# GpSimd writes each weight slot's low part in pieces of 512 columns

## The reference, cut to what matters

```python
# first_block, twice: a mixer (an HGRN2 scan in layer 0, latent attention in layer 1),
# attention over a memory of 256 tokens, and a gated feed-forward with a short convolution
h = rms_norm(x, mix_norm_g[layer])
z = h @ w_in                                   # hg_w_in or mla_w_in
x = x + concat([mixer(z), memory_attention(z, mem)]) @ w_out[layer]
u = conv(rms_norm(x, ffn_norm_g[layer]) @ w_up[layer]) + conv_b
x = x + (silu(u[..., :2816]) * u[..., 2816:]) @ w_down[layer]
# second_block, once: three branches off one projection
p = (rmsnorm(x, norm_g) * (1 + sc) + sh) @ w_in + b_in
y_a = (a_b * short_conv(a_c * a_x) * silu(a_z)) @ w_br_a
y_f = (fourier_mix(f_u) * silu(f_z)) @ w_br_f
y_c = (neighbourhood_attention(q, k, v, k_ctx, v_ctx, rpb) * silu(c_z)) @ w_br_c
out = rmsnorm(x + gt * ((sig(g_a)*y_a + sig(g_f)*y_f + sig(g_c)*y_c) @ w_out), final_g)
```

## Time and profile before

| | |
|---|---|
| median of three runs | 1850.66 us (1849.72 to 1851.76) |
| span of the profiled execution (the profiler's own time of it) | 1846.5 us |
| TensorE busy | 1809.0 us, 98% |
| VectorE busy | 931.2 us, 50% |
| ScalarE busy | 731.6 us, 40% |
| GpSimd busy | 690.4 us, 37%, in 217 instructions |
| of it L1201 | 609.0 us in 144 instructions, 4229 ns each |
| HBM traffic | 92 GB/s on average |

### The profile page before, as it was taken

The page is one execution under the profiler, slowest core; times in us unless marked ns, Lnnn a source line. Parts: engine busy times, 40 slices in busy tenths (PEclk is TensorE's granted clock), DMA queues, the critical chain, the costliest instruction groups (busy, mean ns, idle before and its releaser), DMA issues.

```text
span 1846.5 us, 24566 instructions
## 1 busy us (share of the span) xinstructions
PE 1809.0 (98%) x9607; PEld 1472.4 (80%) x9607; DVE 931.2 (50%) x1303; ACT 731.6 (40%) x963; POOL 690.4 (37%) x217
## 2 busy tenths in 40 slices
PE   9999989999999999999999999999999999999998
PEld 6799857888888887566888888888887788888886
DVE  5366874555652116664455655235327734413564
ACT  4152163555554224553355555323214542221423
POOL 1214803444443443330344443444334334443332
PEclk9999999999999999999999999999999999999999
DMA  8632202232222231120232222323421122323211
GB/s 299 245 137 69 70 1 69 93 110 92 91 91 87 94 121 60 36 69 24 69 114 91 91 93 91 109 102 107 82 90 46 46 88 83 117 91 106 77 69 69
DMA packets 28186, 170.35 MB, mean 92 GB/s; under 512 B 3024, under 2 KB 5328, under 8 KB 11728
## 3 DMA queue, kind: packets, MB, share of 16 engines
q1 hardware_dynamic: 24720, 151.20, 23.8%
q10 hardware_dynamic: 3392, 18.09, 2.9%
HBM read 167.18 MB, written 2.10 MB: 92 GB/s over the span
## 4 chain that ended last, share of the span: by engine, by line
PE 76%; issue 11%; DVE 5%; POOL 3%; ACT 3%; DMA 0%; ACTq 0%; POOLq 0%; DVEq 0%
PE ps L397 47%; PE ps L826 12%; POOL wlo L1201 3%; PE ps L682 1%; PE ps L1092 1%; PE ps L1075 1%; PE ps L551 1%; PE ps L553 1%; PE ps L552 1%; PE ps L1104 1%; PE ps L1102 1%; PE ps L1103 1%; PE ps L417 1%; PE ps L917 1%; PE ps L419 1%
## 5 line engine op out<-in xcount | busy, mean ns | idle before, releaser
L1201 POOL TENSOR_TENSOR wlo<-wraw,whi 128x2048 fp32r<-128x2048 f32 (+3 forms) x144 | 609.0, 4229 | 1035.2 <-ACT whi L1316 1011.5
L397 PE MATMUL ps<-hh,whi 128*128 128x512 f32 x1344 | 526.5, 392 | 1.2 <-DVE wlo L1879 0.4
L397 PE MATMUL ps<-hh,wlo 128*128 128x512 f32 x1344 | 523.2, 389 | 0.0
L397 PE MATMUL ps<-hl,whi 128*128 128x512 f32 x1344 | 523.1, 389 | 0.0
L1316 ACT ACTIVATE whi<-wraw 128x2048 fp32r<-128x2048 f32 (+3 forms) x149 | 265.2, 1780 | 361.0 <-PE ps L397 289.0
L397 PEld LDWEIGHTS ps<-hh,whi 128*128 128x128 f32 x1344 | 252.3, 188 | 56.4 <-issue 2.5
L397 PEld LDWEIGHTS ps<-hh,wlo 128*128 128x128 f32 x1344 | 252.3, 188 | 52.7
L397 PEld LDWEIGHTS ps<-hl,whi 128*128 128x128 f32 x1344 | 252.4, 188 | 52.1 <-issue 0.5
L2185 DVE SCALAR_TENSOR_TENSOR scr<-ps,vec,scr 128x510 f32<-128x510 f32 (+1 forms) x176 | 120.2, 744 | 93.1 <-ACT scr L1525 93.1
L826 PE MATMUL ps<-gh,whi 128*128 128x512 f32 x352 | 137.7, 391 | 1.3 <-DVE gl L2200 1.3
L826 PE MATMUL ps<-gh,wlo 128*128 128x512 f32 x352 | 137.0, 389 | 0.0
(11 more groups left out here) (472 smaller groups left out, 2814.1 us busy)
## 6 DMA issues: line engine op xcount, KB each, us to landing
wraw<-in_w SPq DMA_DIRECT2D x63, 1024.0 KB, 4.9
wraw<-in_w0b SPq DMA_DIRECT2D x26, 1024.0 KB, 4.9
wraw<-in_w1o SPq DMA_DIRECT2D x26, 1024.0 KB, 4.9
wraw<-in_wd SPq DMA_DIRECT2D x32, 704.0 KB, 4.0
ada<-in_wada ACTq DMA_DIRECT2D x12, 1024.0 KB, 8.6
xtok<-in_x SPq DMA_DIRECT2D x4, 512.0 KB, 8.6
out<-ytok SPq DMA_DIRECT2D x4, 512.0 KB, 4.0
wraw<-in_w SPq DMA_DIRECT2D x3, 576.0 KB, 3.9
```

Of the source, the lines that this page charges most:

```text
L397: last = mm(o, l, r, start=(k == 0 and n == 0), stop=(k == K - 1 and n == 2))
L1201: nc.gpsimd.tensor_tensor(wlo[:, s % 2, 0:wd], wraw[:, s % 2, 0:wd], whi[:, s % 2, 0:wd].bitcast(F32), ALU.subtract).then_inc(lo_ready, 1)
```

## The change

The low part of a slot is made by several instructions of at most 512 columns: four for 2048 columns, three for 1408 and 1152, two for 1024. They follow one another with no wait between, and the last one adds to `lo_ready`. VectorE's low parts stay whole.

```diff
+LOW = 512
@@ in block.gpsimd, lo(s, i=None, wd=SLOT) @@
                 pool.wait_ge(hi_ready, n)
-                nc.gpsimd.tensor_tensor(wlo[:, s % 2, 0:wd], wraw[:, s % 2, 0:wd], whi[:, s % 2, 0:wd].bitcast(F32),
-                                        ALU.subtract).then_inc(lo_ready, 1)
+                for a in range(0, wd, LOW):
+                    b = min(a + LOW, wd)
+                    last = nc.gpsimd.tensor_tensor(wlo[:, s % 2, a:b], wraw[:, s % 2, a:b], whi[:, s % 2, a:b].bitcast(F32),
+                                                   ALU.subtract)
+                last.then_inc(lo_ready, 1)
```

## The result

The changed kernel takes 1856.29 us (median of 7 runs, 1853.38 to 1856.70) where the kernel before, beside it, takes 1849.72 (1848.35 to 1851.76): a ratio of 1.0030, 95% interval 1.0021 to 1.0040. A second set of runs gave 1854.64 (11 runs, 1853.05 to 1856.74) against 1849.89, a ratio of 1.0027 (1.0018 to 1.0036). It is slower, by 6.6 and 4.8 us; 1856.5 was predicted.

A forecast was written before the change was run, and what follows sets the result against it. TensorE, busy 1809.0 of 1846.5 us, was taken to bound the kernel. Gains of 5.0 us against losses of 10.75 add 5.8 us to the span; with 4.2 us from span to median that predicts 1856.5 us, range 1848 to 1864.

The forecast's parts named there:

- GpSimd's price: Splitting a full 2048-column low part into four instructions costs GpSimd 0.35 us more, bounds 0 and 0.6 us.
- Turns: At piece boundaries VectorE and GpSimd alternate, one instruction each; each SBUF-only VectorE instruction delays the low part 0.25 to 0.55 us.
- The rival without turns: VectorE never gets in between pieces; nothing won, just-in-time slots pay the bare price: 5.5 us slower, 1856.2 us, chance 0.2.
- pieces cost nothing extra: Rival: pieces are free but take turns; losses 6.3 us against 6 of gains, 1851 us, no measurable change, chance 0.25.
- off the path by its own row: Reading of the profile before: GpSimd, busy 37%, is not on the path that sets the time.
- `mkn` near 819: L2319 from 815.37 waits only for piece 2, so TensorE's 1.22 us wait on mkn goes: 1.2 us won.
- `pr`: L2445 at 1386.09 is done at 1387.25 instead of 1389.27, so TensorE's wait goes whole: 1.3 us won.
- `mqn`: TensorE's wait on mqn near 743 goes: 0.7 us won.
- the table chain: Sine tables, stalls at 693.37 and 702.02: each chained instruction pays a piece; 0.5 us won, bounds -1 and +2.
- the softmax after 819: Stall at 825.95 of two short prm instructions shortens the softmax chain some 1.5 us; waits on prm give 1.0 us.
- Slot 144: Inverse transform's sums: L2518, L2519, L2520 take turns with pieces 2 to 4; low part ends 1729.5, not 1727.13: 2.3 us lost.
- Slots 21 and 73: Just-in-time low parts where VectorE's instructions now take turns between the pieces: each 1.3 us late, 2.6 us lost together.

The follow-up runs named there:

- the first experiment: Changed kernel with the low part left whole in the twenty slots it reaches just in time, the rest in pieces: 1842.93 us, ratio to before 0.9957.
- the six-slot kernel: Pieces of 512 columns in slots 61, 64, 65, 69, 70 and 119 alone, every other low part one instruction: 1844.53 us, ratio to before 0.9971.

## Why the prediction was right

The mechanism was right, in both its halves and nearly slot by slot. That the first median, 1856.29 us, came within 0.2 us of the figure is luck all the same: the work itself costs 4.6 us and not 5.8, and half-clock stretches, which no step counted, made up the rest.

**GpSimd's price.** Predicted 0.35 us per full slot, measured 0.42 (slots 20 and 72: +0.42 each). Pieces start 1.25 us apart, where I had 1.23. The low parts' own busy time rose by 102 us and not by 44: the 44 left out the turns, which count as GpSimd's now.

**Turns.** They take one each, back to back, with no wait and no signal between the pieces: chain and slots above show it at every place. The rival without turns gave the same time, 1856.2, and is refuted by the traces and by the first experiment, which by it couldn't have been faster than before. That pieces cost nothing extra is refuted by slot 20. Of the signs named in advance, L2518 (here L2522) fell to 1.78 us and not to 1.7 or less, the waits on `wlo` at slots 21, 73, 106 and 108 are 0.5 to 0.9 us and not 1 or more, and the one on `mkn` is down to 0.4 and not gone. One reading was loose: "off the path by its own row" goes by GpSimd's busy share, while the page of before has L1201 with 3% in its chain that ended last. They are twelve low parts between 1480 and 1722 us, and in that stretch my list of losses lacked slots 124 to 130. The Trainium skill (SBUF — State Buffer, section "Who interferes with whom") says that two SBUF inputs or a two-port mode take the pair of ports shared with GpSimd for a whole instruction, and that an instruction with at most one SBUF input outside those modes does not contend. The trace agrees with the second half too: L2150, with one input in PSUM, takes 0.69 us beside the last piece of slot 21, as it does with GpSimd idle (0.68 at 327.34 before), where L1878 and L1860 took 1.73 and 1.77.

**Gains, 5.0 predicted, 5.7 found.** `mkn` near 819 1.2 and 1.40; `pr` 1.3 and 1.36; `mqn` 0.7 and 1.00; `mkn` near 756 0.3 and 0.36; the table chain 0.5 and 0.85, four turns in each stretch as told; the softmax after 819 1.0 and 0.71, the one I had too high.

**Losses, 10.75 predicted, 10.3 found.** Slot 144 2.3 and 2.28. Slots 106, 108, 110 and 112 0.7, 0.7, 0.45, 0.75 and 0.64, 0.68, 0.45, 0.61; 100 to 104 0.6 and 0.75; 140 0.7 and 0.77; 12 0.6 and 0.72. Two terms were off. Slots 21 and 73 lost 0.90 each and not 1.3: the low part grew by 1.32 us as worked out, but TensorE came 0.42 later from slot 20 and the low part's start did not, so it had that much more in hand. Two late slots in a row don't simply add. And slots 10 and 150 lost nothing (150 did lose 0.33 in the kernel with only twenty slots in pieces), 124 to 130 lost 0.36 that I had not listed, 134 0.39 for 0.25.

**The sum and the clock.** Without the clock the change costs 4.6 us, where I had 5.8. The 4.2 us that I put between span and median were two things: a run's time lies some 2.0 us above its own span, and the profiled execution of before (span 1846.5) was one of the fastest, some 1848.5 by this, at a mean clock of 0.997. Taking the two together did no harm, since it led back to the median. What came on top is half-clock stretches, of which I had counted none: two in the trace of before, three in the second of the changed kernel, four in the first (near 164, 280, 847 and 1734). The one behind slot 144's wait is in both traces of the changed kernel; the first has the one at 164 beside it, and a median 1.65 us higher than the second set's.

## What to carry to other kernels

Cutting a GpSimd instruction in pieces doesn't free VectorE, it hands out turns: each VectorE instruction that contends waits out one piece, and each turn delays what waits for GpSimd by that instruction's own length, on top of 0.14 us per added piece. So cut only where a VectorE stall ends in a TensorE wait (here six slots, 7.5 us below before with pieces of 256), leave whole what is just in time, and look for both kinds in the trace before choosing one size for all. Count the slack per slot at the point where TensorE comes, since a stall one slot earlier adds to it.

## What the runs showed of the hardware

TensorE's clock has stretches of some 3.4 us, in two traces one of 6.8, at the lower of its two levels (granted 0.5, 1.2 GHz). Which of them a run has differs from run to run: eleven of the twelve traces have one near 280, behind a gap of 2.2 us between two matmuls' starts that all twelve have, eight have one near 840, and three one near 164, though all twelve have the same gap of 2.1 us before it. The trace of before has two, near 277 and 840, which its 40 slices of 46 us average away. With slot 144's wait of 2.65 us TensorE stood still, and then worked at half clock: 11 matmuls in 4 us instead of 19. Windows of the first profiled execution of the changed kernel, and of the kernel with slots 69 and 119 whole, whose wait was 2.68 us (columns: us, then busy us and count of PE, PEld, DVE, ACT and POOL, granted clock, DMA share, GB/s):

```profile
1734.00:1738.00 4.00, 4.00 (x11) 3.12 (x12) 3.41 (x4) 0.90 (x2) 4.00 (x3) 0.57 0.76 244
```

```profile
1734.00:1738.00 4.00, 4.00 (x19) 3.31 (x18) 2.45 (x3) 1.06 (x1) 4.00 (x4) 1.00 0.74 260
```

Of the six traces with this wait (2.6 to 4.1 us) five have such a stretch behind it, of the six others none. With 256 columns a second one follows the 2.6 us wait near 1288, and in the six-slot kernel one follows the 2.8 us wait at 712, where the kernel before waits 3.2 us and has none. So such waits make it likelier and don't settle it; one costs 1.6 us. The times of a kernel's runs fall in groups about that far apart: the second set of the changed kernel has three runs at 1853.1, five at 1854.5 to 1854.9 and three at 1856.5 to 1856.7. In the 21 runs of before beside the first experiments the mean time at a mean clock of 0.995, 0.996 and 0.997 was 1851.1, 1849.5 and 1848.1 us, in the two later sets 1851.1 to 1851.3, 1849.7 to 1849.8 and 1848.8 to 1848.9. So most of the spread goes with the clock, though single runs don't sort by it (one at 0.996 took 1847.73).
